# The sixteenth expert's output of the first layer is weighted and summed by TensorE from SBUF, with the overflow tile's, in place of a store and gathers

## What is computed

```python
for e in range(MOE_EXPERTS):
    hdn = jax.nn.silu(x @ w_gate[e]) * (x @ w_up[e])
    y = y + combine[:, e:e + 1] * (hdn @ w_down[e])
...
x = x + g2 * y[:n_lat].reshape(b_, t_len, d_)
ctx = ctx + cg2 * y[n_lat:].reshape(b_, c_len, d_)
```

## Time and profile before

| | us |
|---|---|
| median of 3 runs | 1086.82 (1085.74 to 1088.62) |
| profiled execution | 1080.25 |
| its span | 1078.3 |
| PE busy | 976.4 |
| DVE busy | 619.7 |
| ACT busy | 181.9 |
| POOL busy | 92.5 |

### The profile page before, as it was taken

One profiled execution on the slowest core, in us unless ns is written; L12 is line 12 of the kernel. 1 busy time (PEld: TensorE's weight loads), 2 busy tenths in 40 slices (PEclk: granted clock), 3 DMA queues, 4 the chain that ended last, 5 costly groups with the idle time before them and its releaser, 6 DMA issues.

```text
span 1078.3 us, 19613 instructions
## 1 busy us (share of the span) xinstructions
PE 976.4 (91%) x7956; PEld 583.2 (54%) x7956; DVE 619.7 (57%) x1496; ACT 181.9 (17%) x348; POOL 92.5 (9%) x139
## 2 busy tenths in 40 slices
PE   3899999999999799999999974997997999978885
PEld 1333433447545599888978842443645554534432
DVE  1200599745924696776675525538516977755653
ACT  2200013036203300000000013314613000000001
POOL 4300000000100110000002014000010100000000
PEclk9899999998999899999999995999998899999999
DMA  9999958853021589999999999543223799999993
GB/s 340 397 402 387 383 202 315 305 209 145 5 78 54 204 312 374 411 387 397 402 383 409 426 374 355 202 156 156 79 81 117 295 355 407 399 391 411 421 426 145
DMA packets 65225, 315.34 MB, mean 292 GB/s; under 512 B 6359, under 2 KB 7991, under 8 KB 52496
## 3 DMA queue, kind: packets, MB, share of 16 engines
q1 hardware_dynamic: 52128, 283.64, 67.7%
q0 software_dynamic: 7728, 18.30, 4.9%
q10 hardware_dynamic: 5312, 12.59, 3.0%
HBM read 303.81 MB, written 17.17 MB: 298 GB/s over the span
## 4 chain that ended last, share of the span: by engine, by line
PE 66%; DMA 21%; DVE 7%; SPq 2%; ACT 2%; issue 2%; ACTq 0%; POOL 0%; PEldq 0%; DVEq 0%; POOLq 0%
PE ps L554 45%; DMA ring<-in_moe_w_gate 15%; PE ps L978 8%; DMA ring<-in_even_w_in 3%; PE ps L567 3%; PE ps L876 3%; DMA ring<-in_ada_w 2%; PE ps L1010 2%; SPq L471 2%; PE ps L1073 1%; PE ps L1268 1%; PE ps L810 1%; DMA y_rows<-ar 1%; DMA xh<-y_rows,sm 1%; DVE xh L1724 0%
## 5 line engine op out<-in xcount | busy, mean ns | idle before, releaser
L554 PE MATMUL ps<-ring,ar 128*32 128x384 f32 (+6 forms) x3888 | 487.4, 468 | 28.3 <-DMA ring<-in_moe_w_gate 17.3
L554 PEld LDWEIGHTS ps<-ring,ar 128*32 128x32 f32 (+2 forms) x3888 | 202.9, 121 | 163.9 <-issue 98.9
L978 PE MATMUL ps<-ring,ar 128*32 128x128 f32 x1488 | 165.2, 273 | 0.0
L978 PEld LDWEIGHTS ps<-ring,ar 128*32 128x32 f32 x1488 | 162.0, 110 | 1.8
L2001 DVE STREAM_TRANSPOSE ar<-ar 32x256 f32<-32x256 f32 x304 | 132.1, 435 | 4.4 <-issue 0.2
L554 PE MATMUL ps<-xh,ring 128*128 128x512 f32 x256 | 115.6, 607 | 2.2 <-DMA ring<-in_even_w_in 2.1
L2037 DVE TENSOR_TENSOR ar<-ar,ps 128x384 f32<-128x384 f32 (+2 forms) x33 | 15.9, 482 | 136.4 <-PE ps L978 68.3
L554 PE MATMUL ps<-ring,xh 128*128 128x512 f32 x192 | 87.4, 612 | 1.8 <-ACT xh L1344 1.6
L554 PEld LDWEIGHTS ps<-xh,ring 128*128 128x128 f32 x256 | 48.8, 194 | 67.2 <-issue 66.6
L2162 DVE SCALAR_TENSOR_TENSOR ar<-ar,cpar 128x512 f32<-128x512 f32 x120 | 79.6, 745 | 0.0
L567 PE MATMUL ps<-ring,silu_c 128*32 128x512 f32 x384 | 49.3, 633 | 21.6 <-DMA ring<-in_ada_w 21.6
(11 more groups left out here) (333 smaller groups left out, 920.2 us busy)
## 6 DMA issues: line engine op xcount, KB each, us to landing
ring<-in_moe_w_down SPq DMA_DIRECT2D x33, 2048.0 KB, 25.4
ring<-in_moe_w_gate SPq DMA_DIRECT2D x32, 2048.0 KB, 19.3
ring<-in_moe_w_up SPq DMA_DIRECT2D x31, 2048.0 KB, 15.1
ring<-in_ada_w SPq DMA_DIRECT2D x24, 2048.0 KB, 20.1
ring<-in_even_w_in SPq DMA_DIRECT2D x5, 2048.0 KB, 18.2
y_rows<-gm POOLq DMA_DIRECT2D x17, 384.0 KB, 14.1
ring<-in_odd_w_in SPq DMA_DIRECT2D x3, 2048.0 KB, 16.3
y_rows<-ar ACTq DMA_DIRECT2D x16, 288.0 KB, 8.9
```

The source lines that it names most:

```text
L554: return nc.tensor.matmul(o, l, r, start=start, stop=stop)
L978: m = nc.tensor.matmul(ps[96:128, bank, g * P:(g + 1) * P], xgT[:, p, c, 32 * g:32 * g + 32], w[:, c, 3 * P:HID], start=c == 0 and g == 0, ...
```

## The change

Tile 15 (`FULL_TILE`) is no longer stored or gathered; its output stays in the odd half of `yb`, and TensorE multiplies it by a second matrix, `full_mix`, and adds the overflow tile's part on top in PSUM. VectorE makes the second table beside the first. The counters are waited for at 256 and 224 (`Y_STORED`), that is for tiles 14 and 13. The overflow tile's down product goes to another bank, and further overflow tiles, if there were any, use the even half of `yb`.

```diff
+        last_mix, full_mix = view(M_H2, 512), view(M_H2 + 512, 3, 512)
+        LAST, FULL_TILE = NEXP, NEXP - 1
+        Y_STORED = (16 * NEXP, 16 * (NEXP - 2))
+        LAST_Y_BANK = 2
...
                 if b == ("oin", 0, 2):
                     for p in range(2):
-                        sp.wait_ge(sem(f"y_stored{p}"), 256)
+                        sp.wait_ge(sem(f"y_stored{p}"), Y_STORED[p])
...
             def last_turned():
                 pe.wait_ge(sem("mix_src"), 1)
                 for j in range(NT):
                     for q in range(4):
-                        m = mm(ps[32 * q:32 * q + 32, 7, j * P:(j + 1) * P], last_hot[:, j, :], ident)
+                        mm(ps[32 * q:32 * q + 32, 4, j * P:(j + 1) * P], last_hot[:, j, :], ident)
+                for j in range(NT):
+                    nc.tensor.transpose(ps[0:96, 7, j * P:(j + 1) * P], slot_hot[:, j, 0:96], ident)
+                    for g, b in enumerate((7, 5, 6)):
+                        m = mm(ps[96:P, b, j * P:(j + 1) * P], slot_hot[:, j, 32 * g:32 * g + 32], ident)
...
             def mix_rows(j):
-                if j == 0:
-                    pe.wait_ge(sem("y_dve"), NE[0])
                 if j >= 2:
                     pe.wait_ge(sem("mix_taken"), j - 1)
                 b, cols = 4 + 2 * (j % 2), slice(j * P, (j + 1) * P)
+                mm(ps[:, b, :], full_mix[0:96, 0, cols], yb[0:96, 1, 0:512])
+                mm(ps[:, b + 1, 0:256], full_mix[0:96, 0, cols], yb[0:96, 1, 512:768])
+                for g in range(3):
+                    m = nc.tensor.matmul(ps[:, b + 1, 256:512], full_mix[96:P, g, cols], yb[96:P, 1, 256 * g:256 * g + 256],
+                                         start=False, stop=g == 2, skip_group_check=True)
+                m.then_inc(sem("mixed"), 1)
+                if j == 0:
+                    pe.wait_ge(sem("y_dve"), NE[0])
                 for half in range(2):
-                    if half:
-                        pe.wait_ge(sem("mixed"), 2 * j + 1)
+                    pe.wait_ge(sem("mixed"), 3 * j + half + 1)
                     for q in (half, 2 + half):
                         part = slice(32 * q, 32 * q + 32)
-                        m = mm(ps[:, b + q // 2, 256 * half:256 * half + 256], last_mix[part, cols], yb[part, 0, 0:256])
+                        m = nc.tensor.matmul(ps[:, b + q // 2, 256 * half:256 * half + 256], last_mix[part, cols],
+                                             yb[part, 0, 0:256], start=False, stop=True, skip_group_check=True)
...
             def y_half(e, p):
...
                 A_(*y_copy(p, 0), ACT.Copy).then_inc(sem("y_act"), 1)
+                if isinstance(e, int) and e == FULL_TILE:
+                    return
...
             def last_taken():
...
-                A_(last_mix, ps[:, 7, :], ACT.Copy).then_inc(sem("mix_src_taken"), 1)
+                A_(last_mix, ps[:, 4, :], ACT.Copy).then_inc(sem("mix_src_taken"), 1)
+                A_(full_mix[0:96, 0, :], ps[0:96, 7, :], ACT.Copy).then_inc(sem("mix_src_taken"), 1)
+                for g, b in enumerate((7, 5, 6)):
+                    A_(full_mix[96:P, g, :], ps[96:P, b, :], ACT.Copy).then_inc(sem("mix_src_taken"), 1)
...
                 def last_added(j):
-                    dve.wait_ge(sem("mixed"), 2 * j + 2)
+                    dve.wait_ge(sem("mixed"), 3 * j + 3)
...
+                    V.tensor_scalar(full_w, R["tile"], float(FULL_TILE), None, ALU.is_equal)
...
+                    link(V.tensor_tensor(direct, last_w, full_w, ALU.add))
+                    link(V.scalar_tensor_tensor(not_now, R["tile"], float(EARLY), direct, ALU.is_lt, ALU.add))
...
+                    link(V.tensor_tensor(full_w, full_w, sm[:, 0:2 * NT], ALU.mult))
+                    link(V.tensor_tensor(last_hot, slot_hot[:, :, 0:NARROW], last_w.unsqueeze(2).to_broadcast([P, 2 * NT, NARROW]),
+                                         ALU.mult))
+                    hot = slot_hot[:, :, 0:CAP[0]]
+                    link(V.tensor_tensor(hot, hot, full_w.unsqueeze(2).to_broadcast([P, 2 * NT, CAP[0]]), ALU.mult))
+                    V.tensor_tensor(last_hot[:, 0:NT, :], last_hot[:, 0:NT, :], last_hot[:, NT:2 * NT, :], ALU.add)
+                    V.tensor_tensor(hot[:, 0:NT, :], hot[:, 0:NT, :], hot[:, NT:2 * NT, :], ALU.add)\
                         .then_inc(sem("mix_src"), 1)
...
             def y_gathered():
                 for p in range(2):
-                    pool.wait_ge(sem(f"y_stored{p}"), 256)
+                    pool.wait_ge(sem(f"y_stored{p}"), Y_STORED[p])
```

40 lines of the change are left out of this document (18 added, 22 removed).

## The result

The changed kernel takes **1096.91 us** (median of 4 runs, 1095.12 to 1099.85), the kernel before 1087.13 beside it (1085.74 to 1088.62). The ratio is 1.0111, 95% interval 1.0072 to 1.0151: slower by 1.1%; the medians differ by 9.8 us, 0.9%. The forecast was 1085.8 us with a range of 1082.0 to 1090.8, "within 0.3%" at 0.58. It was wrong: the time lies outside the range, and the change costs where a slight gain was forecast. Medians are over all runs of a session, ratios leave out the slow runs (1106.42 and 3991.33 us of the change in two later sessions, 1298.18 of the kernel before in one), which moves no median by 1 us.

A forecast was written before the change was run, and what follows sets the result against it. DMA engines bound the experts of both layers; between them the chain through combining layer 0's outputs counts. 1.9 us gained there, 0.9 lost at the head: -1.0 from 1086.82 gives 1085.8 us, range 1082.0 to 1090.8.

The forecast's parts named there:

- Step 1: Combination of layer 0's outputs: late gathers wait for tile 14's store instead of tile 15's and move up 3.9 us.
- Rival C: Late gathers start only behind the early gather in their shared queue; slower, 1092.3 us; chance 0.08.
- Step 2: Five added mixing matmuls per token block on TensorE: 2.66 us plus about 0.3, taken as 2.5 net behind block 1.
- TensorE ends last there: At block 0, VectorE's addition waits for TensorE's mixing until 655.0, so it gains 3.2 us, not 3.9.
- rival A: Added matmuls overlap, blocks 2 and 3 cost 1.6 each, backlog covers the head; faster, 1082.5 us; chance 0.22.
- Step 3: TensorE's clock is full from about 654 and stays so; first unit 7.1 us, block 1's transposes gain 6.9.
- rival B: Clock stays at half through mixing and first unit; slower, 1090.6 us; chance 0.10.
- Step 4: Mixing of blocks 2 and 3 lengthens each of two cycles by 2.5 us, leaving 1.9 us of the gain.
- term of 5.0: Microseconds given back in the two cycles that hold the mixing of blocks 2 and 3.
- Step 5: Head of layer 0's experts: building matrices makes TensorE 3.2 us late; backlog covers 2.3, 0.9 is lost.
- remaining 2.3 go into TensorE's own waits for loads: In layer 0's experts, 2.3 of TensorE's 3.2 us delay disappears in its waits for loads.

The follow-up runs named there:

- useless matmuls at expert 1: Kernel before plus five unneeded f32 matmuls of 512 columns on TensorE ahead of the matrices at expert 1; 1089.17 us, ratio 1.0052.
- plain layout: The change with tile 15's 1024 columns left on 96 partitions, two mixing matmuls a block, second table later; 1086.58 us over 96 rows, 1086.94 over 128.
- late useless matmuls: Kernel before plus five unneeded f32 matmuls of 512 columns on TensorE behind expert 14's gate product; 1085.61 us, ratio 1.0022.
- late tables: The change with tile 15's matrices turned and copied at experts 14 and 15 instead of ahead of expert 1; 1100.79 us, ratio 1.0117.

## Why the prediction was wrong

**Step 1, what the gathers wait for: the number right, the wait wrong.** Forecast 3.9 us. The addition for block 0 has 38.03 us from the last load instead of 41.83: 3.8. Removing store and gathers alone moved block 3 by 4.4 and the time by 4.9 (from 1087.4 of the kernel before to 1082.46). But the late gathers did not start behind tile 14's store: GpSimd waits by the kernel's own code for the early ones (16.02 us), and these landed 1.4 us later than the store. Counted from the last load, the late gathers of block 0 were issued 2.95 earlier, and the second took 6.18 us instead of 7.03; only together do these make 3.8. So the agreement is in part luck. Rival C had the early gather as the holder, but by the shared queue; since GpSimd issues a block's late gathers only when its early ones have landed, no run here tests what the queue alone would do.

**Step 2, the added mixing: the size about right, its place harmless at block 0.** Forecast 2.96 a block (2.66 + 0.3), taken as 2.5 net, bounds 1.6 and 3.1; the added part takes 3.0. "TensorE ends last there" failed in all three profiles: VectorE's addition follows its own weighted sum. By the Trainium skill (TensorE: Matmul & The Clock Gate, Part 3) matmuls on different row groups run side by side. Three 32-row matmuls right behind two 96-row ones took 1.56 us, more than the 3 x 0.44 of the serial price, and those over 128 rows, which can't lie beside anything, 1.46: this case shows no such gain, and rival A falls with it.

**Step 3, "it stays there": failed.** I had the clock full from 654 because TensorE worked without a break, and the first unit at 7.1 us. It took 8.93, 9.30 and 9.72 in the three profiles of the change, and block 1's transposes gained 2.9 to 4.9 instead of 6.9. Full it was through both blocks' mixing in the first and the third profile (9.2 us at 1.00, from 659.3 in the first), so few rows at work don't bring the clock down at once. But VectorE came later than TensorE, which idled 3.07 and 5.57 us where I had 2.0, and the clock was down within a us of the mixing's end at 668.4, not at the end of an idle stretch:

```profile
667.00:668.00 1.00, 0.93 (x6) 0.53 (x8) 0.97 (x2) 0.00 (x0) 0.64 (x1) 1.00 1.05 399
668.00:669.00 1.00, 0.44 (x4) 0.04 (x2) 0.96 (x2) 0.24 (x1) 0.57 (x1) 0.75 1.01 393
```

In the second profile, with hardly any idle time (0.41), it fell inside the mixing. The earlier trace rows showed a clock that falls behind an idle stretch, and I made "busy keeps it full" of it. The Trainium skill (TensorE: Matmul & The Clock Gate, Why this matters for your kernels) has the same rule, to leave no long idle gaps between bursts of matmuls; the stretches at 687 to 693 us above differ, with a clock of 0.50 behind an engine busy for 0.93 of each us and more. The earlier trace rows held the warning: 8 us of narrow products and 32-row matmuls had left the clock at half, which I named under rival B and gave 0.10.

**Step 4, "each grows by 2.5": failed by the clock.** Cycles grew by 3.8 and 3.7 (10.14 and 10.25 to 13.91 and 13.90), together 7.4. Taken over 128 rows they grew by 1.9 and 1.8. So the matmuls' share of a cycle is 1.9 at full clock, below my 2.5 (a part of the added 3.0 went into waits that were there before), and the other 1.9 comes with the small row counts: 1.3 to 1.7 in the unit, the rest in the mixing, which is 4.4 to 4.7 us long instead of 4.2. The term of 5.0 was short by 2.4.

**Step 5, "its backlog is 2.3, so 0.9 is lost for good": failed; 3.3 to 4.1 was lost.** TensorE's work was a little larger than priced: from the first of the matrices' matmuls to expert 1's first product it is 4.73 us instead of 1.12, so 3.6 more and not 3.2, and the load behind it was issued 4.0 later. What the transfers lost can be added up from the DMA shares (1 less the share, over stretches of 3 us from the first load on): 1.1 us before and 3.6 in the change over the first 30 us, 0.9 and 1.7 over the next 15, 1.7 and 1.6 over all the rest. So of the 4.0 the backlog covered 1.5 at the first hole, not 2.3. The second hole, which wasn't looked at, cost 0.8 more: 418.70 came 10.58 us after its neighbour and was just covered, and a stream that is late by 4 us there runs dry a second time (share 0.66).

My "remaining 2.3 go into TensorE's own waits for loads" had it backwards. Up to 550 us TensorE has no such waits (busy for 120.00 of the 120 us from 430 to 550 in both kernels), and 32 loads in a row, from the third on, are issued 4.0 us later. The first wait for gate weights is at 561.12 before and at 571.94 in the change. From there the transfers set the pace, and a transfer that starts late ends late. The useless matmuls at expert 1 lost 3.4 in the same way.

The sum by its own steps, to block 3: forecast +0.9 - 6.9 + 5.0 = -1.0; the first profile of the change +3.7 - 4.9 + 7.4 = +6.2. The difference of 7.2 is the head's 2.8, the first unit's 2.0 and the two cycles' 2.4. Behind block 3 little differs: from there to the load that follows layer 1's first freed buffer it is 143.86 us before and 143.68 and 143.88 in the first two profiles of the change (146.26 in the third). From block 3 to the end of the span it is 379.8 and 381.2 us in two profiles of the kernel before, 381.6, 381.1 and 384.1 in three of the change. So 6.2 to 8.3 of the profiles stand beside 7.9 to 9.8 of the medians; what makes up the rest is not shown.

## What to carry to other kernels

Price added work on a busy engine by where it delays the next transfer: at the start of a stage whose end the DMA engines bound, look through every later hole of the load stream before counting on a backlog, and remember that slack at the end of a stage can be spent only once. Look in the code for every wait ahead of an instruction that you want to move up, not only for the one that comes last today. Count matmuls over part of the array as a threat to the clock of what follows, even where TensorE never pauses; fewer and longer matmuls from a plain layout, over 96 rows as over 128, were 9 us better here than five short ones to a block, together with a cheaper head. An edit whose gain and costs are each near 5 us needs each part switched off by itself, since the parts were easy to measure and the sum hid them.

## What the runs showed of the hardware

- **TensorE's clock falls without an idle engine.** Behind 4.5 us of mixing over 96 and 32 rows it was at half for 3.4 us (units 8.4 to 8.8 us); behind the same columns over 128 rows it stayed full (7.13). Behind 3.3 us of mixing, 96 or 128 rows, it stayed full too. Once at half, it stayed there through 16.65 us of unbroken 96- and 32-row matmuls, and was back within 4 us where these ran over 128 rows (0.61 in 668 to 669, 1.00 from 669). But 9.2 us of the same 96- and 32-row mixing ahead of the first unit ran at full clock in two profiles, and the clock fell within a us behind it; in a third it came back from half while 96-row matmuls ran (0.50 in 651 to 652, 0.96 in 652 to 653). Whether rows, length or both decide isn't settled beyond these cases.
- **A wait that the profile doesn't name lies under the wait for the last weights.** Where TensorE came late enough not to wait for these, it stood all the same: 3.76 us ahead of the narrow down product with late useless matmuls, 4.37 in the plain layout over 96 rows, and 4.07 inside the product, behind its 19th record of 32, with late tables, each time with "issue" as the releaser. The other profiles name the load for 4.2 to 4.9 us. In the first of these cases VectorE's hidden values and their transposes fill 2.0 of the 3.76 us; the last 1.7, and all of the 4.07, have no owner. An earlier load alone may then gain little there; that and what the wait is weren't tried.
